# Two-half loads of three experts' up weights, and a ScalarE copy moved ahead of a root, in a fused encoder step

## The reference

```
for l in range(DEPTH):                      # DEPTH = 2
    ...                                     # attention, memory attention
    x = layernorm(DN_ALPHA * x + mix, ln1_g[l], ln1_b[l])
    for e in range(N_EXPERTS):              # 16 experts, D_EXPERT = 512
        h = jax.nn.silu(t @ w_gate[e]) * (t @ w_up[e])
        y = y + gate[:, e:e + 1] * (h @ w_down[e])
    x = layernorm(DN_ALPHA * x + y, ln2_g[l], ln2_b[l])
# ahead of layer 1:  kv = x @ w_kv_shared ; memory K/V: mem_prompt @ w_mem_kv[l]
```

## Time and profile before

| | us |
|---|---|
| median of 3 runs | 913.7 (913.56 to 913.7) |
| the profiled execution | 912.49 |
| its span, first to last instruction | 910.7 |
| TensorE matmul busy | 789.8 (87%) |
| VectorE busy | 334.0 (37%) |
| ScalarE busy | 187.0 (21%) |
| DMA, mean over the span | 300 GB/s |

### The profile page before, as it was taken

One profiled execution on the slowest core, in us unless ns is written; L12 is line 12 of the kernel. 1 busy time (PEld: TensorE's weight loads), 2 busy tenths in 40 slices (PEclk: granted clock), 3 DMA queues, 4 the chain that ended last, 5 costly groups with the idle time before them and its releaser, 6 DMA issues.

```text
span 910.7 us, 9956 instructions
## 1 busy us (share of the span) xinstructions
PE 789.8 (87%) x3943; PEld 387.3 (43%) x3943; DVE 334.0 (37%) x749; ACT 187.0 (21%) x452; POOL 44.3 (5%) x59
## 2 busy tenths in 40 slices
PE   6998998989899878786879989989999997787775
PEld 4675776453433222222334667655534332222221
DVE  1125554553332121213370254564443242121138
ACT  1214343010321110100110044711004111111101
POOL 1201000003000000000200000000020000000020
PEclk9999998999999999998989999989799999999998
DMA  9832019367999999999797150681689999999991
GB/s 356 309 115 89 1 32 421 148 277 244 424 430 421 429 422 429 424 425 424 220 393 241 64 200 1 278 324 40 260 289 423 430 426 429 422 430 420 430 393 56
DMA packets 43168, 272.95 MB, mean 300 GB/s; under 512 B 5946, under 2 KB 10752, under 8 KB 25456
## 3 DMA queue, kind: packets, MB, share of 16 engines
q1 hardware_dynamic: 32032, 243.69, 65.3%
q0 software_dynamic: 5504, 20.09, 6.3%
q10 hardware_dynamic: 5584, 8.51, 2.6%
HBM read 255.35 MB, written 18.36 MB: 301 GB/s over the span
## 4 chain that ended last, share of the span: by engine, by line
PE 61%; DMA 26%; DVE 9%; ACT 2%; issue 1%; ACTq 0%; SPq 0%; DVEq 0%
DMA arena<-in_expert_w_up 25%; PE bank L917 16%; PE bank L859 6%; PE bank L931 5%; PE bank L1177 5%; PE bank L846 3%; PE bank L1050 3%; PE bank L1098 2%; PE bank L833 2%; PE bank L680 2%; PE bank L778 2%; PE bank L940 1%; PE bank L826 1%; PE bank L687 1%; DMA arena<-in_x_sample 1%
## 5 line engine op out<-in xcount | busy, mean ns | idle before, releaser
L917 PE MATMUL bank<-arena 128*64 128x512 f32 x1024 | 241.3, 629 | 51.9 <-DMA arena<-in_expert_w_up 50.1
L917 PEld LDWEIGHTS bank<-arena 128*64 128x64 f32 x1024 | 77.4, 144 | 212.7 <-issue 147.8
L931 PE MATMUL bank<-arena 128*64 128x512 f32 x512 | 116.9, 599 | 16.7 <-DVE arena L1826 16.7
L1826 DVE COPY arena<-bank 128x256 f32<-128x256 f32 x32 | 13.5, 423 | 276.2 <-PE bank L924 276.2
L1379 ACT ACTIVATE arena<-bank 128x256 f32<-128x256 f32 x32 | 12.3, 383 | 270.3 <-PE bank L917 270.3
L931 PEld LDWEIGHTS bank<-arena 128*64 128x64 f32 x512 | 34.1, 137 | 77.4 <-issue 54.6
L1834 DVE RECIPROCAL arena<-arena 128x256 f32<-128x256 f32 x32 | 56.1, 1753 | 1.1
L859 PE MATMUL bank<-arena 128*128 128x512 f32 x128 | 56.0, 596 | 0.0
L1177 PE MATMUL bank<-arena 128*128 128x512 f32 x96 | 44.1, 621 | 6.6 <-ACT arena L1484 5.7
L1235 ACT COPY arena<-bank 128x512 f32<-128x512 f32 (+2 forms) x30 | 15.8, 536 | 106.7 <-PE bank L680 74.7
L859 PEld LDWEIGHTS bank<-arena 128*128 128x128 f32 x128 | 24.0, 190 | 29.6 <-issue 29.5
(11 more groups left out here) (273 smaller groups left out, 864.2 us busy)
## 6 DMA issues: line engine op xcount, KB each, us to landing
arena<-in_expert_w_gate SPq DMA_DIRECT2D x32, 2048.0 KB, 23.4
arena<-in_expert_w_up SPq DMA_DIRECT2D x32, 2048.0 KB, 28.1
arena<-in_expert_w_down SPq DMA_DIRECT2D x64, 1024.0 KB, 29.8
arena<-in_w_out SPq DMA_DIRECT2D x4, 2048.0 KB, 9.5
expert_rows<-arena ACTq DMA_DIRECT2D x60, 128.0 KB, 7.7
arena<-in_w_kv_shared SPq DMA_DIRECT2D x3, 2048.0 KB, 10.9
arena<-in_w_mem_kv SPq DMA_DIRECT2D x2, 2048.0 KB, 21.3
arena<-sorted_rows POOLq DMA_DIRECT2D x2, 2048.0 KB, 9.7
```

The costliest lines, as they stand in the source:

```text
L917: last = mm(bank[j][64 * half:64 * half + 64, :].rearrange("p (u f) -> p u f", u=2), slots[:, k, 0:CAP], w[:, :, k, 256 * half:256 * half ...
L931: last = mm(bank[3 + j][64 * n:64 * n + 64, :], hid_t[:, j, c, 64 * half:64 * half + 64], w[:, half, c, 512 * n:512 * n + 512], start=(hal ...
```

## The change

Two things are changed; the arithmetic stays.

1. The up weights of experts 3, 4 and 15, in both layers, are loaded in two halves of k (k 0 to 3 and k 4 to 7, of gate and up each). TensorE signals `half_done` when the up product of expert 0, 1 or 12 is through its first half, and SyncE then issues the first half of the new expert into the half of the buffer that is left; the second half follows at `up_done` as before. TensorE waits for the second half in the middle of the up product of these experts. Both halves of the down weights have semaphores of their own now, and TensorE waits for the second one in the middle of each expert's down product.
2. Between the layers ScalarE copies the second `memkv1` tile (into `mem_raw1` and `mem_v1`) ahead of the root of tile 1 instead of behind it.

```diff
+        def halved(e):
+
+            return e in (3, 4, NE - 1)
...
-            def load_up(l, e, buffer, s):
+            def load_up(l, e, buffer, s, k0=0, k1=KC):
 
                 for u, name in enumerate(("expert_w_gate", "expert_w_up")):
                     src = ins[name][l][bass.ds(e, 1)].rearrange("o (p k) f -> (o p) k f", k=KC)
-                    sp.dma_start(buffer[:, u], src).then_inc(s, 16)
+                    sp.dma_start(buffer[:, u, k0:k1], src[:, k0:k1]).then_inc(s, 16)
+
+            def load_next_up(l, e):
+
+                to, s = ups[e % 3], up_in[e % 3]
+                if halved(e + 3):
+                    sp.wait_ge(half_done, half_marks(l, e))
+                    load_up(l, e + 3, to, s[0], 0, KC // 2)
+                sp.wait_ge(up_done, NE * l + e + 1)
+                if halved(e + 3):
+                    load_up(l, e + 3, to, s[1], KC // 2, KC)
+                else:
+                    load_up(l, e + 3, to, s[0])
...
-                    sp.dma_start(dn[j][:, h], src[bass.ds(e, 1), :, h].rearrange("o p c n -> (o p) c n")).then_inc(s, 16)
+                    sp.dma_start(dn[j][:, h], src[bass.ds(e, 1), :, h].rearrange("o p c n -> (o p) c n")).then_inc(s[h], 16)
...
                     if what == "up" and e + 3 < NE:
-                        sp.wait_ge(up_done, NE * l + e + 1)
-                        load_up(l, e + 3, ups[e % 3], up_in[e % 3])
+                        load_next_up(l, e)
...
-            def expert_up(j, w, slots):
+            def expert_up(j, w, slots, second=None, left=False):
 
                 for k in range(KC):
+                    if second and k == KC // 2:
+                        pe.wait_ge(*second)
                     for half in range(2):
...
+                    if left and k == KC // 2 - 1:
+                        last.then_inc(half_done, 1)
                 return last
...
-            def expert_down(j, w):
+            def expert_down(j, w, second=None):
                 for half in range(2):
+                    if second and half:
+                        pe.wait_ge(*second)
...
-                    root(2 * l + 1, t)
+                    if t != 1:
+                        root(2 * l + 1, t)
                     if l == 0 and t < 2:
                         k, b = next(memkv1)
                         own(nc.scalar.copy(mem_raw1[:, 0, k, :], b[:, 0:MW]))
                         out_of(nc.scalar.copy(mem_v1[:, k, :], b[:, MW:2 * MW]))
+                    if t == 1:
+                        root(2 * l + 1, t)
```

More of the change, by code:

```diff
@@ L288, in encoder_step @@
         w_in = {n: sem("w_" + n) for n in ("mem0", "mem1", "ina", "uq", "ukv", "out0", "kvs0", "kvs1", "kvs2", "inb", "out1")}
-        up_in = [sem(f"up_in{b}") for b in range(3)]
-        dn_in = [sem(f"dn_in{j}") for j in range(3)]
+        up_in = [[sem(f"up_in{b}_{i}") for i in range(2)] for b in range(3)]
+        dn_in = [[sem(f"dn_in{j}_{h}") for h in range(2)] for j in range(3)]
         proj_ready = sem("proj_ready")
@@ L406, in loads, with second_halves, half_marks @@
             return l * len(range(e % 3, NE, 3)) + e // 3 + 1
+        def halved(e):
+            return e in (3, 4, NE - 1)
+        def second_halves(l, e):
+            return sum((m, f) <= (l, e) and f % 3 == e % 3 and halved(f) for m in range(DEPTH) for f in range(NE))
+        def half_marks(l, e):
+            return sum((m, f) <= (l, e) and halved(f + 3) for m in range(DEPTH) for f in range(NE - 3))
         def stores(l, e):
@@ L547, in experts @@
                 sp.wait_ge(o_ready, sum(NS[:l + 1]))
-                load_up(l, 1, ups[1], up_in[1])
+                load_up(l, 1, ups[1], up_in[1][0])
                 if l == 1:
@@ L551, in experts @@
                 sp.wait_ge(proj_ready, job_end(before_gu1))
-                load_up(l, 2, ups[2], up_in[2])
+                load_up(l, 2, ups[2], up_in[2][0])
                 load_down(l, 2, 2, dn_in[2])
@@ L570, in experts @@
                     load_up(l, 0, gu[0], ov[l]["ov_w"])
-                    load_down(l, 0, 0, ov[l]["ov_w"])
+                    load_down(l, 0, 0, [ov[l]["ov_w"]] * 2)
                     with sp.Fori(1, NE) as e:
@@ L574, in experts @@
                         load_up(l, e, gu[0], ov[l]["ov_w"])
-                        load_down(l, e, 0, ov[l]["ov_w"])
+                        load_down(l, e, 0, [ov[l]["ov_w"]] * 2)
                     sp.wait_ge(ov[l]["ov_y"], (PASSES - 1) * NE)
@@ L964, in up @@
                 def up(e):
-                    pe.wait_ge(up_in[e % 3], 32 * loads(l, e))
+                    pe.wait_ge(up_in[e % 3][0], 32 * loads(l, e))
                     if e < 2:
@@ L971, in up @@
                         pe.wait_ge(xg_ready, (NE - 2) * l + e - 1)
-                    expert_up(e % 2, ups[e % 3], xg[:, e % 2]).then_inc(up_done, 1)
+                    expert_up(e % 2, ups[e % 3], xg[:, e % 2],
+                              (up_in[e % 3][1], 32 * second_halves(l, e)) if halved(e) else None,
+                              e + 3 < NE and halved(e + 3)).then_inc(up_done, 1)
                 def down(e):
@@ L979, in down @@
                     pe.wait_ge(ht_copied, at)
-                    pe.wait_ge(dn_in[e % 3], 32 * loads(l, e))
+                    pe.wait_ge(dn_in[e % 3][0], 16 * loads(l, e))
                     if e > 1:
@@ L986, in down @@
                         pe.wait_ge(y_copied, copied(l - 1, NE - 2 + e))
-                    expert_down(e % 2, dn[e % 3]).then_inc(down_done, 1)
+                    expert_down(e % 2, dn[e % 3], (dn_in[e % 3][1], 16 * loads(l, e))).then_inc(down_done, 1)
                 keep_warm(bank[1], 512)
```

4 lines of the change are left out of this document (2 added, 2 removed).

## The result

| | before | changed | changed, run again | predicted |
|---|---|---|---|---|
| median, us | 913.2 (14 runs) | 906.7 (14 runs, 900.3 to 912.7) | 904.8 (12 runs, 901.4 to 914.2) | 905.8 |
| ratio to before, 95% interval | | 0.9929 (0.9908 to 0.995) | 0.992 (0.9891 to 0.9948) | 0.9914 |
| profiled execution, us | 912.49 | 900.28 | 905.35 | 904.6 |
| its span | 910.7 | 898.5 | 903.5 | |
| its mean granted clock | 0.957 | 0.966 | 0.956 | |

The change makes the kernel 6.5 us faster (0.7%), within the predicted range and 1.4 us short of the predicted gain of 7.9. The profiled execution of the changed kernel is the fastest of its 14, so its trace overstates the gain: 12.2 us. I use both.

What follows compares the result with a forecast made beforehand. Expert stages were taken as bound by DMA weight bytes, the seam between layers by TensorE's waits. Terms 6.3 + 0.7 + 0.5 + 1.0 - 0.6 = 7.9 us off 912.49 gave 904.6, as median 905.8 us; range 900.5 to 910.5.

Steps and rivals of the forecast that it cites:

- Early halves: Expert stage starts: issuing first halves of experts 3 and 4 early gains 0.5 us in layer 0, 1.0 in layer 1.
- the 8 KB pieces: Weight loads of halved experts: smaller pieces per partition cost 0.3 us a layer, 0.6 in all.
- The rows' delay: Expert stage starts: sorted rows land at about 235 and 687, idling TensorE 2 and 4 us, at no cost.
- Rivals 1 and 2: Sorted rows beside early weights: either they starve, 927 us, chance 8%, or come late by turns, 909 us, chance 14%.
- rival 2: Sorted rows taking turns with weights land late and overrun the cover by some 3 us: 909 us, chance 14%.
- Expert 15's up product: End of layer 0's experts: two halves at the high clock, second from 420.7, down 15 ending at 433.4 instead of 439.4.
- The way over the store: Between the layers: last store lands at 440.2, the gather starts at 441.0, 2.8 us earlier.
- The K/V projection's start: Between the layers: the shared K/V projection waits for weights, not ScalarE, and starts at 458.8, 6.3 us earlier.
- Its clock: Shared K/V projection between the layers: no gain from a higher TensorE clock granted; the bound was +2.4 us.
- rival 3: TensorE's clock gain at the K/V projection is real and the DMA ramps merge: 902 us, chance 20%.
- End of layer 1: Kernel's end: VectorE's final sums wait for the fourth gather and end at 894.7 instead of 895.4, 0.7 us gained.
- The sum: Whole kernel: 6.3 + 0.7 + 0.5 + 1.0 - 0.6 = 7.9 us gained.

Runs made afterwards that it cites:

- e1_copy: The kernel before with only the ScalarE copy moved ahead of the root of tile 1; 909.0 us, ratio 0.9963.
- e4_kvs: e3_late without SyncE's wait for the first gathered tile ahead of the first shared K/V weight load; 905.6 us, ratio 0.9907.
- e5_warm: e4_kvs plus 7 matmuls with unused results in TensorE's idle times between the layers; 904.7 us, ratio 0.9913.
- e6_down: e3_late with TensorE waiting for both halves of the down weights ahead of each down product; 906.9 us, ratio 0.9927.
- e10_warm: e5_warm with SyncE's wait for the first gathered tile ahead of the K/V weights put back; 904.2 us, ratio 0.9924.
- e3_late: The changed kernel with the up weights of experts 3 and 4 whole again, only expert 15's in halves; 906.1 us, ratio 0.9927.
- e7_rows: e3_late with SyncE holding expert 3's up weights until the sorted rows have landed; 910.6 us, ratio 0.9961.
- e8_before: The kernel before, run once more unchanged for a second trace; 912.4 us, ratio 1.0012.
- e2_halves: The changed kernel with the ScalarE copy put back behind the root, leaving the halves alone; 912.3 us, ratio 0.9992.

## Why the prediction was right, point by point

**Early halves: wrong in sign, small in size.** The text says "I take **+0.5 and +1.0**" for reordering, and 0.6 for the 8 KB pieces. The streams are 0.4 and 0.3 us longer in all. The gain was sized by the empty part ahead of the stream and by the missing bytes of the slow stretch, as if that were a ramp paid only once. The empty part was out of reach, since the first weight packet comes 3.7 us behind its issue. The slow stretch is there in either order: 332 and 326 GB/s before, 286 and 284 now. The lower bound, a loss of 2 us or more, was wrong as well: sharing did not slow the whole rows load, as the windows from 220 to 228 show (417 and 396 GB/s). Right was the base of the argument, that the queue is not idle and bytes are only reordered.

**The rows' delay: right in direction, too large.** Expected at 235 and 687 with 2 and 4 us of idle time; they landed at 233.0 and 673.0, that is 18.8 and 18.5 us behind up 0, with 0.25 us and none; in the second trace up to 3.0. The stream did not notice even those. Rivals 1 and 2, the starving and the late rows, did not happen. Still, 2.3 MB took 16.8 us from its issue at 216.3, about what rival 2 worked out for equal turns with 8 KB pieces (16.5). With the rule of the Trainium skill that rival 2 quoted (DMA: Bandwidth & Descriptors, Queues, rings and completion order), that a DMA engine takes turns between queues by the packet, the trace agrees so far: from 224 to 228 the weights' queue moved 146 packets with 1.07 MB and the rows' queue 134 with 0.52 MB, about equal turns. What did not follow is the rival's 909: the delay stayed under its cover.

**Expert 15's up product: right.** Two runs of 3.6 us, the second from 421.25 (420.7 predicted), the high clock; down 15 ends at 434.1 (433.4 predicted, 439.4 before). The first run starts at 417.07 and not at 415.6, since TensorE was still busy with down 13; that costs nothing, as the second waits for its bytes.

**The way over the store: right.** Store landed at 440.5 (440.2), gather at 441.27 (441.0), against 443.79 before. Behind up 0 it is 2.0 to 2.7 us earlier (2.8 predicted). The store does pay for the busy queue: 5.12 us instead of 2.39. The prediction gave the store some 2 us behind the end of the weight stream; it is 0.7 us behind it, at a stream end 1.4 us later than the 438.4 taken.

**The K/V projection's start: right.** Weights landed at 458.6, start 458.69 (458.8 predicted); behind up 0 it is 5.8 and 6.2 us earlier. It waits for weights and no longer for ScalarE.

**Its clock: this term was left out, and it came.** The text granted no gain, since TensorE would be idle for 5 of the 6 us before. It isn't: the memory projection starts 1.3 us later than thought and takes 2.7 us longer, ends at 456.5 instead of 452.5, and the turns of the tile follow, so TensorE stands only 1.3 us ahead of the K/V projection. The low clock moved to a place where it is covered. 2.4 us more in the trace; `e1_copy`, `e4_kvs`, `e5_warm`, `e6_down` and `e10_warm` show 20.84 (or 20.8) too, `e3_late` and `e7_rows` 22.5, behind 3.3 and 3.1 us of idle time. This is half of rival 3's mechanism, the half on the clock, and it is in part luck: it hangs on how long TensorE happens to stand ahead of the K/V projection.

**End of layer 1: right in mechanism, too small.** Down 15's landing to the end is 26.1 and 25.1 instead of 27.5: 1.4 and 2.4 us, where 0.7 was predicted. The rest is the gather, which the prediction had taken as fixed. The fourth gather lands 5.5 and 4.5 us behind the last weights; before it was 6.3 and 5.6. It is issued 2.5 us ahead of that landing (869.85 against 872.39), 5.35 us in the second trace, instead of 1.6 (881.59 against 883.18). GpSimd starts these gathers when expert 13's rows are stored, and down 13 runs ahead of up 15, so expert 15's halves are not what moves them. In the second trace up 14 ran in 7.09 us instead of 8.78, which brings down 13 forward. For the 0.8 us of the first trace no cause is shown.

**The sum.** Predicted 7.9. By the traces: seam 8.2 to 8.6, of which the start 5.8 to 6.2 and the clock 2.4, end 1.4 to 2.4, stream -0.7; some 9.5 in all. The medians give 6.5 to 7.3. The predicted sum lies between the two in part because its misses offset each other: the early halves were put at +0.9 with their pieces and gave -0.7, while the clock's 2.4 was put at nothing and the end was put 0.7 to 1.7 too low. Between traces and medians 2 to 3 us are left. Such an amount lies within what single traces stray: the profiled executions of before are 0.7 and 1.4 us below their medians and the changed kernel's 6.5 us below and 0.6 above, each median is uncertain by 2 us, and the clock ahead of layer 1's experts alone moves a trace by 3.4 us. A lower share of executions with the high clock under the K/V projection would do it too, but only profiled executions show that. Which it is stays open.

## What to carry to other kernels

Where the DMA engines are full, an earlier issue moves no end: look for stretches with a DMA share well below 1 and fill those, and measure a stream from the first moment at which it can run to its last landing. At the end of such a stream it helps to halve the last load, because the first half's work is done before the last bytes land; follow that gain over the next store and the next gather to see how much arrives. Here 4.7 to 5.0 us at down 15 became 2.0 to 2.7 at the gather, and in the medians it shows, if at all, only together with the copy (0.9929 and 0.992 against 0.9963 for the copy alone, with intervals that overlap). A copy that frees an accumulator bank should not stand in its engine's order behind a wait for another engine, and if it does, the cost can be more than the wait, since TensorE can lose its clock in it (here 3.9 us of start and 2.4 of clock). Where a stretch hangs on several waits of about the same length, take one more trace of the same kernel before a difference of a few microseconds is explained.

## What the runs showed of the hardware

**A DMA issued into a full queue waits for its first bytes.** In `e7_rows`, where the weights are issued when the rows have landed, their first packet starts 0.95 us behind the issue. Issued 0.8 to 1.7 us behind the rows, in the kernels with early halves, it starts 3.2 to 3.9 us behind it.

**The end of a GpSimd load of rows is slow, and not by sharing alone.** In `e7_rows`, with nothing beside it, the load ends with 133 GB/s at a DMA share of 0.53, which is 251 GB/s for a full share; the two windows ahead of it have 397 and 402. Beside weights the same end shows as 4 us at 284 to 332 GB/s with a DMA share above 1, with 8 KB pieces of weights (286, 284) or 16 KB (332, and 294 in `e8_before`). The weights' packets are slow in it too: in the changed kernel 146 of them take 70.3% of the engines' time from 224 to 228, 0.31 us each, and 126 take 80.6% from 228 to 232, 0.41 us each. Why, no run here tells.

**The clock fell after short pauses.** In the changed kernel TensorE stood 1.80 and 1.35 us around its last transposes ahead of the memory projection, and this ran at the low level in part (16.70 us instead of 13.97); in `e2_halves` the pauses were 2.16 and 0.98 us (17.00 us). Before, pauses of 1.93 and 0.99 us in the same place left it at the high level. So it is in all traces: the four of kernels with expert 15 whole kept the clock here, the seven with it in halves and nothing added lost it. With five matmuls put between them (`e5_warm`, `e10_warm`) it ran at the high level (13.90). The pauses are so alike that they don't tell what decides it: `e6_down` was busy 1.09 of the 4 us ahead of the projection, as long as before, though in part at the low level, and lost its clock.

**A late up 0 need not cost.** In `e8_before` the route ahead of layer 1's experts ran at the low clock. TensorE's timelines of `e8_before` and of before:

```profile
653.83 10.37 PE L940 MATMUL bank<-arena 128*128 128x512 f32 x12 [0.57 <-DVE arena L1789]
```

```profile
655.21 6.00 PE L940 MATMUL bank<-arena 128*128 128x512 f32 x12 [0.83 <-DVE arena L1789]
```

4.4 us more for the same 12. But GpSimd issued the rows at 665.6, ahead of up 0 (667.1), and the last landing came 214.7 us behind up 0 instead of 219.1. From the issue of the rows it is 216.2 and 215.9: the stage hangs on the rows and the weight stream, and TensorE's delay was absorbed. The difference of 4.4 us between the two traces of before, in the table of segments, is this and not the change.
